# A two-row product with a long contraction, spread over four strips of output partitions

## The chip, the cores and the metric

The kernel runs on one core of one Trainium2 chip. The metric is device time in microseconds (us). Of each version several executions are timed, and one execution is profiled.

## The reference

Two transformer blocks are computed one after the other on 256 tokens of width 1024, all in float32. The first has three mixers (latent attention "MLA", gated linear attention "GLA", attention over a memory) and a feed-forward part; the second is modulated by a conditioning vector. The change touches only the modulation of the second block:

```python
mod = jax.nn.silu(c) @ w_mod[l] + b_mod[l]
shift1, scale1, gate1, shift2, scale2, gate2 = jnp.split(mod[:, None, :], N_MOD, axis=-1)
n_mod_c = 2 if last else N_MOD
mod_c = jax.nn.silu(c_ctx) @ w_mod[l, :, :n_mod_c * D_MODEL] + b_mod[l, :n_mod_c * D_MODEL]
mods_c = jnp.split(mod_c, n_mod_c)
h_c = ctx * (1.0 + mods_c[1]) + mods_c[0]
...
h = x * (1.0 + scale1) + shift1
```

`w_mod` is 1024 x 6144. Its first 2048 columns are wanted for two vectors (`c` and `c_ctx`), the other 4096 for one.

## The kernel before

Every engine has its own program, and semaphores tie them together. The order of the work on each engine is written out by hand.

**Weight panels.** A panel is 512 columns of a weight matrix. It goes through in units of two blocks of 128 rows: SP loads a unit into `raw` (a ring of four), ACT rounds it to `whi` (line 1228), DVE takes the rest as `wlo` (line 1645), and PE (line 703) multiplies both with the split activations into one of two `acc` banks. One unit is 12 matmuls with 512 columns each. ACT and DVE run three units ahead of PE.

**Modulation panels.** The 6144 columns of `w_mod` are 12 panels. POOL loads each in four pieces into `wm` (line 599), one piece as soon as `mod_free` says that it was used; loads of the first five panels stand ahead of POOL's rotary work in its program. `sic` holds both conditioning vectors as columns (128 partitions, 8 blocks for each). The first four panels are done on PE by `mod_panel`: for each of the 8 blocks of the contraction, a matmul with the two columns of `sic` as its stationary side and 128 x 512 of `wm` as its moving side adds into partitions 0 and 1 of a PSUM bank (`turned`). DVE copies the two rows to `modrow` (`mod_row`, line 1732), PE turns them into columns (`mod_turn`, four transposes with 2 x 128 as the stationary side, line 788), and DVE adds the bias (`mod_out`, lines 1766 and 1767). The other eight panels are summed on DVE (`mod_sum_tile`) and PE turns their sums by matmuls with 128 x 128 as the stationary side and a column of ones, `one_col`, as the moving side (`mod_columns`, line 1030).

**Where the first four panels stand.** They lie in the loop of the GLA stage, over nine steps s = 0 to 8. On PE a step is: wait until `gla_in` is s; eight score matmuls of 128 columns each (line 897, step 1 line 889); two units of the panels Q1, Q2, G20, G21 (not in step 8); then `mod_panel(s // 2)` in the odd steps and `mod_turn(s // 2 - 1)` in the even ones from 2 on. On DVE a step s is: a split (line 1645), `decayed(s)` (lines 2025 and 2027, it needs the scores of step s - 1 and ACT's exponential for s, and signals `gla_in`), `weights(s - 1)` (line 2043, two masked copies), `exponents(s + 1)` (lines 2009 and 2010), a split, the gates G20 and G21 in steps 6 to 8 (`gate_in_psum` line 1974, `gate_on` line 1983), then `mod_row` in even and `mod_out` in odd steps. ACT's step is a cast, the exponential (line 1390), a cast, an evacuation or a sigmoid (lines 1246 and 1373), and from step 5 on eight sums of squares (line 1411). After the loop come `mod_out(3)` and `weights(8)` on DVE, the products with the GLA values on PE (lines 916 and 917), ACT's root of the query norms (line 1260), the panels UKV0 to UKV3 and the MLA stage.

Of the kernel before, what the change touches and what calls it, by code (L numbers as in the profile page):

```python
# [25 lines left out]
ALU = mybir.AluOpType  # L26
ACT = mybir.ActivationFunctionType
AX = mybir.AxisListType

P = 128  # L30
# [3 lines left out]
KT = D // P  # L34
# [24 lines left out]
COLS = 512  # L59
# [3 lines left out]
class Order:  # L63
# [5 lines left out]
    def done(self, ins):  # L69

        self.n += 1
        ins.then_inc(self.sem, 1)
        self.eng.wait_ge(self.sem, self.n if self.i is None else self.n + self.per * self.i)
# [59 lines left out]
AB_KEYS, AB_QUERIES, AB_OUT = 12, 13, 18  # L133
AB_GATE = 2
MOD_CTX = 4
MOD_LOOP = 3
MOD_UNIT = 3
MOD_DOWN = (2, 8, 17, 21, 26)
# [23 lines left out]
def t_names():  # L162
# [8 lines left out]
    out += g("y", 4) + g("hc", 4) + g("h2", 4)  # L171
    out += [f"WU{c}.{i}" for c in range(8) for i in range(2)] + g("mod", 12)[MOD_CTX:]
    out += g("x2", 4) + g("kA", 2) + g("qA", 2)
# [26 lines left out]
def hybrid_kernel(nc, a, out):  # L200

    ctx = ExitStack()
    with ctx:
        def sem(name):
            return ctx.enter_context(nc.semaphore(name))

        def sb(name, shape, dt=F32, scope=ctx):
            return scope.enter_context(nc.sbuf_tensor(name, shape, dt))
# [3 lines left out]
        tb = [ctx.enter_context(nc.psum_tensor(f"turned{i}", [P, COLS], F32)) for i in range(2)]  # L212
# [8 lines left out]
        ident = sb("ident", [P, P])  # L221
# [5 lines left out]
        modx = sb("modx", [P, 16])  # L227
        ln1c = sb("ln1c", [P, 16])
        x3c = sb("x3c", [P, 16])
        one_col = sb("one_col", [P, 1])  # L230
        sic = sb("sic", [P, 16])
        rot = sb("rot", [P, 2, T, 64])
        bias = sb("bias", [P, 2, COLS])
        wm = sb("wm", [P, KT // UNIT, UNIT, COLS])
        modrow = sb("modrow", [2, COLS])
        turn = sb("turn", [P, 2, COLS])
        prob = sb("prob", [P, 2, COLS])
        probT = sb("probT", [P, 2, COLS])
# [106 lines left out]
        t_free = [sem(f"turned_free{i}") for i in range(2)]  # L345
# [16 lines left out]
        def ev(name):  # L362

            if name not in once:
                once[name] = sem(name)
            return once[name]
# [319 lines left out]
        def _(pe):  # L686
# [28 lines left out]
            def t_begin(name):  # L715
                b, k = T_USE[name]
                pe.wait_ge(t_free[b], k + 1)
                return tb[b], t_full[b]
# [49 lines left out]
            def mod_panel(c):  # L768

                bank, full = t_begin(f"mod.{c}")  # L770
                if c == 0:
                    pe.wait_ge(ev("sic_ready"), 1)
                pe.wait_ge(mod_free, 4 * c + 4)
                for k in range(KT // UNIT):
                    pe.wait_ge(mod_landed[k], 16 * (c + 1))
                    for kk in range(UNIT):
                        kt = UNIT * k + kk
                        ins = pe.matmul(bank[0:2, :], sic[:, kt:kt + KT + 1:KT], wm[:, k, kk],  # L778
                                        start=(kt == 0), stop=(kt == KT - 1))
                    ins.then_inc(mod_free if kt < KT - 1 else full, 1)  # L780

            def mod_turn(c):

                b, k = T_USE[f"mod.{c}"]
                pe.wait_ge(t_free[b], k + 2)
                bank, full = t_begin(f"modt.{c}")
                for j in range(4):
                    ins = pe.transpose(bank[:, 2 * j:2 * j + 2], modrow[:, P * j:P * j + P], ident[0:2, 0:2])
                ins.then_inc(full, 1)

            def lt_wait(name, g=3):
# [31 lines left out]
            s, k = PLAN.bank("AQ")  # L823
            pe.wait_ge(panel_out[s], k + 2)
            bank, full = t_begin("aT")
            for t in range(T):
                ins = pe.transpose(bank[:, P * t:P * t + P], aq[:, t, 0:P], ident[:])
            ins.then_inc(full, 1)
            panel("GQ", lta)
            b, k = T_USE["aT"]  # L830
            pe.wait_ge(t_free[b], k + 2)
            pe.wait_ge(ev("wg_landed"), 16)
            for g in range(2):
                bank, full = t_begin(f"z.{g}")
                for j in range(2):
                    h = 2 * g + j
                    ins = pe.matmul(bank[:, 256 * j:256 * j + 256], wg[0:GATE_RANK, P * h:P * h + P],
                                    aT[0:GATE_RANK, :], start=True, stop=True)
# [10 lines left out]
            for name in ("mqT", "mkT"):  # L849
                b, k = T_USE[name]  # L850
# [27 lines left out]
            for g in ("gqT.0", "gqT.1", "gkT.0", "gkT.1"):  # L878
                b, k = T_USE[g]
                pe.wait_ge(t_free[b], k + 2)  # L880
            qg = ["Q1", "Q2", "G20", "G21"]
            for s in range(9):
# [3 lines left out]
                if s == 1:  # L886
                    bank, full = s_begin("gla.off")
                    for h in range(H_GLA):
                        ins = pe.matmul(bank[:, P * h:P * h + P], lhs[:, h, 0:P], rhs[:, h, P:2 * P],
                                        start=True, stop=True)  # L890
                    ins.then_inc(full, 1)
                else:
                    for t in range(T):
                        bank, full = s_begin(f"gla.{max(s - 1, 0)}.{t}")
                        for h in range(H_GLA):
                            tok = slice(P * t, P * t + P)
                            ins = pe.matmul(bank[:, P * h:P * h + P], lhs[:, h, tok], rhs[:, h, tok],  # L897
                                            start=True, stop=True)
# [7 lines left out]
            for name in ("gla.off", "gla.7.0", "gla.7.1"):  # L906
                b, k = S_USE[name]
                pe.wait_ge(s_free[b], k + 2)
            for t in range(T):
                for g in range(2):  # L910
                    bank, full = t_begin(f"go.{2 * t + g}")
                    for j in range(2):
                        h = 2 * g + j
                        o = bank[:, 256 * j:256 * j + 256]
                        if t == 1:
                            pe.matmul(o, attn[:, 2, h, :], gv[:, 0, 256 * h:256 * h + 256], start=True, stop=False)
                        ins = pe.matmul(o, attn[:, t, h, :], gv[:, t, 256 * h:256 * h + 256],
                                        start=(t == 0), stop=True)
# [8 lines left out]
            for g in range(4):  # L927
                bank, full = t_begin(f"qn.{g}")
                for j in range(2):
                    for t in range(T):  # L930
                        c = 192 * (2 * g + j)
                        ins = pe.transpose(bank[:, 256 * j + P * t:256 * j + P * t + P], q[:, t, c:c + P], ident[:])
# [3 lines left out]
            for g in range(2):  # L936
                bank, full = t_begin(f"qr.{g}")
                for j in range(2):
                    for t in range(T):
                        ins = pe.transpose(bank[:, 256 * j + P * t:256 * j + P * t + P],  # L940
                                           work[:, t, 0:512][:, P * (2 * g + j):P * (2 * g + j) + P], ident[:])
                ins.then_inc(full, 1)
            bank, full = t_begin("kp")
            for t in range(T):
                ins = pe.transpose(bank[:, P * t:P * t + P], kpe[:, t, :], ident[:])
            ins.then_inc(full, 1)
            pe.wait_ge(ev("k_normed"), 1)
            for g in range(4):
                bank, full = t_begin(f"kn.{g}")
                for j in range(2):  # L950
                    for t in range(T):
                        c = 256 * (2 * g + j)
                        ins = pe.transpose(bank[:, 256 * j + P * t:256 * j + P * t + P], kv[:, t, c:c + P], ident[:])
                ins.then_inc(full, 1)
            for g in ("kn.2", "kn.3"):
                b, k = T_USE[g]
# [66 lines left out]
            def mod_columns(c):  # L1023

                bank, full = t_begin(f"mod.{c}")
                n = c - MOD_CTX
                pe.wait_ge(mod_sum, n + 1)
                src = msum[0][:, n] if n < MOD_LOOP else msum[1][:, n % 2]
                for j in range(4):
# [4 lines left out]
            for c in range(2):  # L1034
                for k in range(D_FF // P // UNIT):
                    if c == 0 and k == 2:
                        up_turn(7)
                    n = units_of("WD0") * c + k
                    if 0 <= n - MOD_UNIT < MOD_LOOP:
                        mod_columns(MOD_CTX + n - MOD_UNIT)  # L1040
                    if n == 2 * units_of("WD0") - 1:
# [4 lines left out]
                    if n in MOD_TURN:  # L1046
                        mod_columns(MOD_CTX + MOD_LOOP + MOD_TURN.index(n))
                    if c == 0 and k % 2 == 0:
                        for g in range(2):
                            b, n = T_USE[f"WU{k // 2}.{g}"]  # L1050
# [4 lines left out]
            for k in range(4):  # L1055
                if k == 1:
                    p, n = PLAN.bank("WD1")
# [573 lines left out]
        def _(dve):  # L1631
            order = Order(dve, dve_order)
            done = order.done
# [94 lines left out]
            def mod_row(c):  # L1728

                b, k = T_USE[f"mod.{c}"]  # L1730
                dve.wait_ge(t_full[b], k + 1)
                dve.tensor_copy(modrow[:], tb[b][0:2, :]).then_inc(t_free[b], 1)
                dve.sem_inc(mod_free, 1)

            def mod_sum_tile(total, kt, c):
# [13 lines left out]
            def mod_sums(c, pos):  # L1749

                n = c - MOD_CTX
                if n >= MOD_LOOP + 2:
                    b, k = T_USE[f"mod.{c - 2}"]
# [6 lines left out]
            def mod_out(c):  # L1760

                b, k = T_USE[f"mod.{c}" if c >= MOD_CTX else f"modt.{c}"]
                dve.wait_ge(t_full[b], k + 1)
# [66 lines left out]


            dve.wait_ge(ev("grid_ready"), 1)
            dve.wait_ge(ev("pos_landed"), 16)
            done(dve.tensor_copy(stat[:, 7, 6:8], stat[:, 7, 4:6].bitcast(I32)))
            done(dve.tensor_copy(stat[:, 7, 8:9], stat[:, 7, 2:3].bitcast(I32)))
# [41 lines left out]
            b, k = T_USE["h.3"]  # L1877
# [18 lines left out]
            for g in range(2):  # L1896
                b, k = T_USE[f"z.{g}"]
                dve.wait_ge(t_full[b], k + 1)
                for j in range(2):
                    ins = dve.tensor_scalar(zb[:, 2 * g + j, :], tb[b][:, 256 * j:256 * j + 256],  # L1900
                                            col("b_gla_gate", 2 * g + j), None, ALU.add)
# [24 lines left out]
            b, k = T_USE["ck"]  # L1926
            dve.wait_ge(t_full[b], k + 1)
            for kk in range(2):
                ins = dve.tensor_scalar(turn[:, 0, 256 * kk:256 * kk + 256], tb[b][:, 256 * kk:256 * kk + 256],
                                        col("g_ckv", kk), None, ALU.mult)  # L1930
# [118 lines left out]
            for g in ("gqT.0", "gqT.1", "gkT.0", "gkT.1"):  # L2049
                b, k = T_USE[g]  # L2050
# [47 lines left out]
            for t in range(T):  # L2098
                for h in range(H_GLA):
                    v = r_gla[:, t, DV_GLA * h:DV_GLA * h + DV_GLA]  # L2100
                    ins = dve.scalar_tensor_tensor(v, og[:, t, h], stat[:, 6, 4 * t + h:4 * t + h + 1], v, ALU.mult, ALU.mult)
# [39 lines left out]
            for c in range(2):  # L2141
                name, part = f"WO{c}", slice(COLS * c, COLS * c + COLS)
                p = panel_wait(name)
# [37 lines left out]
            assert cursor[0] == u0 + AHEAD  # L2181
            with dve.Fori(0, MOD_LOOP) as i:
                order.enter(i, KT)
                for c in (1, 2):
# [5 lines left out]
                    up_square(c, i)  # L2190
                order.leave(MOD_LOOP)
            cursor[0] += 24
# [6 lines left out]
            for c in range(2):  # L2199
# [14 lines left out]
                p = panel_wait(name)  # L2214
# [135 lines left out]
            for g in range(2):  # L2350
                b, k = T_USE[f"gate2.{g}"]
# [4 lines left out]
            for half in (slice(0, COLS), slice(COLS, D)):  # L2356
                for t in range(T):
                    ins = dve.tensor_scalar(x[:, t, half], x[:, t, half], stat[:, 1, 2 + t:3 + t], stat[:, 1, 4 + t:5 + t],
                                            ALU.add, ALU.mult)
# [83 lines left out]
```

## Time and profile before

| | |
|---|---|
| median of 3 executions | 1028.32 us (1028.26 to 1030.88) |
| profiled execution, span | 1025.4 us |
| its own time | not recorded apart; the median lies 2.9 us above the span |
| PE busy | 977.8 us (95%) |
| weight loads of PE | 765.0 us (75%) |
| DVE busy | 747.6 us (73%) |
| ACT busy | 551.8 us (54%) |
| POOL busy | 168.8 us (16%) |
| HBM read | 173.33 MB, 170 GB/s over the span |

The span is the time from the first to the last instruction of the profiled execution. PE is TensorE's matmuls, PEld its weight loads, which can overlap them. The chain of waits is followed back from the last instruction: at each step to what released it, or to the instruction before it on its engine. A group of matmuls in the profile counts instructions: a float32 product is two of them, each with a weight load of its own, a transpose is one. Ends of matmuls are modelled, so the time that a row of them takes is read from start to start.

### The profile page before, as it was taken

The page shows a single profiled execution, that of the slowest core. Times are in us where ns is not written, and L with a number is a line of the kernel's source. Part 1 is how long each engine was busy: PE and PEld are TensorE (multiplying, and loading weights), DVE is VectorE, ACT ScalarE, POOL GpSimd, SP SyncE. Part 2 cuts the span into 40 slices and gives each one's busy share as a digit, 9 for nine tenths or more (in the row PEclk, how much of TensorE's full clock was granted, in tenths as well). Part 3 has the DMA queues.
Part 4 walks back from the last instruction along what each step waited for, and adds up shares of the span by engine and source line. Part 5 has one row for each costly group of instructions (what it writes and reads, how often), then busy time and mean ns, then how long its engine had stood idle before and what let it go on. Part 6 is the DMA issues. An engine that isn't in the chain of part 4 may idle for free.

```text
span 1025.4 us, 13780 instructions
## 1 busy us (share of the span) xinstructions
PE 977.8 (95%) x4636; PEld 765.0 (75%) x4636; DVE 747.6 (73%) x1085; ACT 551.8 (54%) x816; POOL 168.8 (16%) x250
## 2 busy tenths in 40 slices
PE   6999999999999999999999999999999799999995
PEld 5787785665867787888888887776777578777784
DVE  5778456676667778887678787666567879999945
ACT  6557545264766445555333336756543467777532
POOL 7000000113600000110112002450000323333400
PEclk9999999999999999999999999999999899999998
DMA  8675454665543156887589555211125355556551
GB/s 257 212 242 164 123 165 155 217 201 156 158 156 108 63 175 211 266 264 242 200 306 339 180 179 191 73 62 62 62 76 183 91 158 169 166 171 218 181 189 41
DMA packets 99746, 175.11 MB, mean 171 GB/s; under 512 B 8252, under 2 KB 36444, under 8 KB 99692
## 3 DMA queue, kind: packets, MB, share of 16 engines
q1 hardware_dynamic: 92460, 148.87, 45.8%
q0 software_dynamic: 7184, 25.50, 7.7%
q8 instruction: 32, 0.52, 0.2%
q14 instruction: 22, 0.18, 0.1%
q10 hardware_dynamic: 48, 0.04, 0.0%
HBM read 173.33 MB, written 1.05 MB: 170 GB/s over the span
## 4 chain that ended last, share of the span: by engine, by line
PE 81%; DVE 10%; ACT 5%; issue 4%; DMA 1%; DVEq 0%; SPq 0%; ACTq 0%
PE acc L703 61%; PE scores L1103 3%; PE turned L778 3%; PE turned L1111 2%; DVE wlo L1645 2%; PE turned L755 2%; PE scores L897 2%; ACT whi L1228 1%; DVE ltb_lo L1685 1%; PE turned L729 1%; PE scores L964 1%; DVE conv L2379 1%; DVE turn L1700 1%; PE scores L963 1%; DVE turn L1703 1%
## 5 line engine op out<-in xcount | busy, mean ns | idle before, releaser
L1645 DVE TENSOR_TENSOR wlo<-raw,whi 128x1024 fp32r<-128x1024 f32 (+2 forms) x270 | 347.1, 1306 | 104.9 <-ACT whi L1228 96.1
L1228 ACT CAST whi<-raw 128x1024 fp32r<-128x1024 f32 (+2 forms) x270 | 273.5, 1030 | 206.6 <-PE acc L703 171.1
L703 PE MATMUL acc<-whi,lta_lo 128*128 128x512 f32 (+2 forms) x576 | 229.0, 398 | 4.5 <-DVE lta_lo L1685 3.6
L703 PE MATMUL acc<-wlo,lta_hi 128*128 128x512 f32 (+2 forms) x576 | 223.2, 387 | 0.0
L703 PE MATMUL acc<-whi,lta_hi 128*128 128x512 f32 (+2 forms) x576 | 223.1, 387 | 0.0
L703 PEld LDWEIGHTS acc<-whi,lta_lo 128*128 128x128 f32 x576 | 108.9, 189 | 39.3 <-issue 13.5
L703 PEld LDWEIGHTS acc<-wlo,lta_hi 128*128 128x128 f32 x576 | 109.0, 189 | 22.4
L703 PEld LDWEIGHTS acc<-whi,lta_hi 128*128 128x128 f32 x576 | 109.0, 189 | 19.9
L703 PE MATMUL acc<-whi,ltb_lo 128*128 128x512 f32 (+1 forms) x272 | 109.7, 403 | 6.8 <-DVE ltb_lo L1685 3.5
L599 POOL DMA_DIRECT2D wm<-in_w_mod x48 | 34.5, 719 | 478.6 <-DVEq L1745 264.8
L703 PE MATMUL acc<-whi,ltb_hi 128*128 128x512 f32 (+1 forms) x272 | 106.7, 392 | 0.0
L703 PE MATMUL acc<-wlo,ltb_hi 128*128 128x512 f32 (+1 forms) x272 | 106.3, 391 | 0.0
L703 PEld LDWEIGHTS acc<-whi,ltb_lo 128*128 128x128 f32 x272 | 52.0, 191 | 23.2 <-DVE ltb_lo L1685 4.9
L1266 ACT ACTIVATE probT<-turned 128x512 f32<-128x512 f32 (+1 forms) x44 | 25.3, 576 | 66.9 <-PE turned L755 66.7
L703 PEld LDWEIGHTS acc<-wlo,ltb_hi 128*128 128x128 f32 x272 | 52.0, 191 | 11.8
L703 PEld LDWEIGHTS acc<-whi,ltb_hi 128*128 128x128 f32 x272 | 52.1, 192 | 10.2
L703 PE MATMUL acc<-whi,ff_lo 128*128 128x512 f32 x128 | 51.3, 401 | 0.0
L703 PE MATMUL acc<-whi,ff_hi 128*128 128x512 f32 x128 | 50.5, 395 | 0.0
L703 PE MATMUL acc<-wlo,ff_hi 128*128 128x512 f32 x128 | 50.5, 395 | 0.0
L703 PE MATMUL acc<-whi,act_lo 128*128 128x512 f32 x88 | 34.9, 397 | 0.1
L703 PE MATMUL acc<-whi,act_hi 128*128 128x512 f32 x88 | 34.8, 395 | 0.0
L703 PE MATMUL acc<-wlo,act_hi 128*128 128x512 f32 x88 | 34.7, 395 | 0.0
(340 smaller groups left out, 1429.5 us busy)
## 6 DMA issues: line engine op xcount, KB each, us to landing
raw<-in_w_in SPq DMA_DIRECT2D x88, 512.0 KB, 4.2
wm<-in_w_mod POOLq DMA_DIRECT2D x48, 512.0 KB, 5.2
raw<-in_w_up SPq DMA_DIRECT2D x88, 256.0 KB, 3.2
raw<-in_w_up SPq DMA_DIRECT2D x32, 512.0 KB, 4.7
raw<-in_w_down SPq DMA_DIRECT2D x32, 512.0 KB, 5.0
raw<-in_w_down SPq DMA_DIRECT2D x44, 256.0 KB, 3.0
raw<-in_w_mem_kv SPq DMA_DIRECT2D x8, 512.0 KB, 6.2
raw<-in_w_o SPq DMA_DIRECT2D x8, 512.0 KB, 3.6
```

Of the source, the lines that this page charges most:

```text
L599: pool.dma_start(wm[:, k], rows(a["w_mod_2"], k)[:, :, bass.ds(COLS * c, COLS)])\
L703: ins = pe.matmul(acc[s][:, t, 0:n], lhs[part][:, kt0 + kk, tok], w[:, u % RING, kk, 0:n], start=(k == 0 and kk == 0 and j == 0), stop=(la ...
L729: ins = pe.transpose(bank[:, 256 * kk + P * t:256 * kk + P * t + P], src[:, t, c:c + P], ident[:])
L755: ins = pe.transpose(bank[:, P * j:P * j + P], prob[:, (STEPS[name][0] + i) % 2, P * j:P * j + P], ident[:])
L778: ins = pe.matmul(bank[0:2, :], sic[:, kt:kt + KT + 1:KT], wm[:, k, kk], start=(kt == 0), stop=(kt == KT - 1))
L897: ins = pe.matmul(bank[:, P * h:P * h + P], lhs[:, h, tok], rhs[:, h, tok], start=True, stop=True)
L963: pe.matmul(o, qnT[:, h, P * t:P * t + P], knT[:, h, 0:P * (t + 1)], start=True, stop=False)
L1103: return pe.matmul(bank[:, :], qT[br][lane, h // 2, P * t:P * t + P], kT[br][lane, h // GROUP, :], start=True, stop=True)
L1111: ins = pe.matmul(bank[:, 0:HD], pT[:, P * kt:P * kt + P], v[:, HD * (h // GROUP):][:, 0:HD], start=(kt == 0), stop=(kt == 3))
L1228: act.copy(whi[:, s, :, 0:n], raw[:, s, :, 0:n]).then_inc(hi_ready, 1)
L1266: act.activation(dst, tb[b][0:(parts or P), 0:n], ACT.Copy, scale=scale).then_inc(t_free[b], 1)
L1645: dve.tensor_tensor(wlo[:, s, :, 0:n], raw[:, s, :, 0:n], whi[:, s, :, 0:n].bitcast(F32), ALU.subtract)\
```

## The change

The matmuls of block kt of a modulation panel write to partitions 32 * (kt mod 4) and the one after it instead of always to partitions 0 and 1. The blocks 0 to 3 start the four sums and the blocks 4 to 7 end them. So a panel ends as four partial sums of two rows each, in partitions 0, 1, 32, 33, 64, 65, 96 and 97. `modrow` is 98 partitions high and `mod_row` copies all 98 rows (of the rows between, whatever the bank holds). `mod_turn` is four float32 matmuls instead of four transposes: the stationary side is 98 x 128 of `modrow`, the moving side is `strips`, 98 x 2 zeros and ones that add the four partial sums. `strips` is built once from the identity by a DVE reduction near the start, and shares a small tile with `one_col`.

```diff
+STRIPS = 4
+STRIP_ROWS = 32 * (STRIPS - 1) + 2
...
-        one_col = sb("one_col", [P, 1])
+        strip_cols = sb("strip_cols", [P, 3])
+        one_col, strips = strip_cols[:, 0:1], strip_cols[:, 1:3]
...
-        modrow = sb("modrow", [2, COLS])
+        modrow = sb("modrow", [STRIP_ROWS, COLS])
...
                         kt = UNIT * k + kk
-                        ins = pe.matmul(bank[0:2, :], sic[:, kt:kt + KT + 1:KT], wm[:, k, kk],
-                                        start=(kt == 0), stop=(kt == KT - 1))
+                        row = 32 * (kt % STRIPS)
+                        ins = pe.matmul(bank[row:row + 2, :], sic[:, kt:kt + KT + 1:KT], wm[:, k, kk],
+                                        start=(kt < STRIPS), stop=(kt >= KT - STRIPS))
...
                 for j in range(4):
-                    ins = pe.transpose(bank[:, 2 * j:2 * j + 2], modrow[:, P * j:P * j + P], ident[0:2, 0:2])
+                    ins = pe.matmul(bank[:, 2 * j:2 * j + 2], modrow[:, P * j:P * j + P], strips[0:STRIP_ROWS, :],
+                                    start=True, stop=True)
...
-                dve.tensor_copy(modrow[:], tb[b][0:2, :]).then_inc(t_free[b], 1)
+                dve.tensor_copy(modrow[:], tb[b][0:STRIP_ROWS, :]).then_inc(t_free[b], 1)
...
             dve.wait_ge(ev("grid_ready"), 1)
+            done(dve.tensor_reduce(strips[:], ident[:].rearrange("p (g c) -> p c g", g=STRIPS)[:, 0:2, :], AX.X, ALU.add))
             dve.wait_ge(ev("pos_landed"), 16)
```

## Rows read from the trace of the kernel before

**Rows 1.** The page: the span, and the chain that ended last, by engine and line.

```profile
span 1025.4 us, 13780 instructions
...
PE 81%; DVE 10%; ACT 5%; issue 4%; DMA 1%; DVEq 0%; SPq 0%; ACTq 0%
PE acc L703 61%; PE scores L1103 3%; PE turned L778 3%; PE turned L1111 2%; DVE wlo L1645 2%; PE turned L755 2%; PE scores L897 2%; ACT whi L1228 1%; DVE ltb_lo L1685 1%; PE turned L729 1%; PE scores L964 1%; DVE conv L2379 1%; DVE turn L1700 1%; PE scores L963 1%; DVE turn L1703 1%
```

**Rows 2.** Chain of waits in the GLA loop and behind it: start us, us, what.

```profile
172.94 6.96 PE turned L778 x16
179.90 1.98 PE scores L897 x16
181.88 5.46 PE acc L703 x24
187.34 0.34 PE turned L788 x4
...
239.59 6.96 PE turned L778 x16
...
251.03 1.96 PE turned L917 x8
```

**Rows 3.** Line 778: durations (least, median, most), first and last start, forms.

```profile
L778 PEld LDWEIGHTS turned<-wm,sic x64: 82/85/86, 172.9 to 245.5; 128*2 128x2 f32 x64
L778 PE MATMUL turned<-wm,sic x64: 592/592/593, 172.9 to 246.0; 128*2 128x512 f32 x64
```

**Rows 4.** Timeline of PE's weight loads inside the first modulation panel.

```profile
172.87 0.09 PEld L778 LDWEIGHTS turned<-wm,sic 128*2 128x2 f32 x2 [0.35 <-issue]
173.30 0.09 PEld L778 LDWEIGHTS turned<-wm,sic 128*2 128x2 f32 x1 [0.34 <-issue]
```

**Rows 5.** Chain of waits around `mod_columns`, and line 1030's weight loads on the timeline.

```profile
492.48 0.79 PE turned L1030 x8
...
495.78 1.09 PEld L1030 LDWEIGHTS turned<-one_col,work 128*128 128x128 f32 x8
```

**Rows 6.** Chain of waits: products of one tile shape (917, 916), and of alternating shapes (963, 964).

```profile
254.38 0.43 PE turned L917 x2
...
299.27 0.63 PE scores L964 x2
```

**Rows 7.** Timeline of DVE, GLA steps 4 to 8.

```profile
202.13 0.68 DVE L1732 COPY modrow<-turned 2x512 f32<-2x512 f32 x1 [6.88 <-PE turned L778]
...
226.34 0.69 DVE L2025 TENSOR_TENSOR arena<-arena 128x512 f32<-128x512 f32 x1 [0.17 <-PE scores L897]
...
234.59 0.69 DVE L2025 TENSOR_TENSOR arena<-arena 128x512 f32<-128x512 f32 x1
...
236.03 1.51 DVE L2043 COPY_PREDICATED arena<-gmask,scores 128x512 f32<-128x512 int8 x2
```

**Rows 8.** Timeline of ACT: the exponential of step 7.

```profile
224.84 1.06 ACT L1390 ACTIVATE arena<-arena 128x1024 f32<-128x1024 f32 x1
```

**Rows 9.** Stages of two loop steps: PE, PEld, DVE, ACT, POOL busy, PEclk, DMA share, GB/s.

```profile
179.90:187.70 7.80, 7.80 (x46) 6.56 (x45) 7.19 (x9) 1.32 (x2) 0.72 (x1) 1.00 0.73 258
187.70:195.10 7.40, 7.40 (x41) 6.16 (x42) 6.67 (x10) 2.79 (x3) 0.00 (x0) 1.00 0.46 142
195.10:202.10 7.00, 7.00 (x18) 1.32 (x17) 0.16 (x1) 2.91 (x3) 2.12 (x3) 1.00 0.72 200
```

**Rows 10.** A DMA issue group of the GLA stage (KB each, us to landing), and one issue on POOL's timeline.

```profile
wm<-in_w_mod POOLq DMA_DIRECT2D x16, 512.0 KB, 5.1
...
199.31 0.72 POOL L599 DMA_DIRECT2D wm<-in_w_mod  x1 [1.00 <-PE turned L778]
```

**Rows 11.** Near the start: a small DVE reduction, DVE's rotary work, ACT's sine.

```profile
L1719 DVE TENSOR_REDUCE stat<-work x8: 220/420/421, 54.1 to 64.1; 128x4 f32<-128x256 f32 x4, 128x1 f32<-128x256 f32 x2, 128x1 f32<-128x64 f32 x2
...
33.67 0.23 DVE L1855 TENSOR_SCALAR rot<-arena 128x128 f32<-128x128 f32 x1
...
37.33 1.28 ACT L1318 ACT_TABLE_LOAD   x1
```

## The prediction

> **What bounds the kernel now.** I first read the page. The chain that ended last is PE for 81% of a span of 1025.4 us, and line 778, the matmuls of the modulation panels, holds 3% of it [rows 1]. So these matmuls are on the path, not beside it. Then I read the chain of waits through the GLA loop [rows 2]. It never leaves PE: scores, two units, panel, scores, two units, turn, and so on, each piece starting where the last one ended. The panel at 172.94 holds the path for 6.96 us and so does the one at 239.59, the last of four of them: 27.8 us. A turn (line 788) holds it for 0.34 us. Behind the loop the chain goes through DVE's last work to the products of line 917 at 251.03. The table by stages says why nothing else shows: in a pair of steps (stages from 179.9 to 202.1) PE has no gap, DVE is nearly full in the steps without a panel (7.19 of 7.80 us) and idle under the panel (0.16 of 7.00) [rows 9]. Whatever shortens the panel is gained at once, until DVE or ACT are late.
>
> **What one panel consists of.** Line 778 is 64 instructions for 32 products [rows 3]: each float32 product is two instructions, each with its weight load. The weight loads come 0.43 us apart [rows 4], and 6.96 / 16 = 0.435 us is what one instruction takes from start to start (its own 592 ns is a modelled end). A weight load takes 85 ns and lies under the running matmul. All 16 use partitions 0 and 1 as output and can only follow each other.
>
> **The panel with four strips.** The number of instructions, their columns and their kind stay; only the output partitions turn. No pair of matmuls in this trace has different output strips, so whether they run side by side isn't shown. Bounds: if they run side by side without limit, four strips share 16 instructions, 4 x 0.435 = 1.74 us; if not at all, 6.96 us; if each change of strip has to empty the array as a change of tile shape does, more. The price of such a change can be read: two instructions with 256 columns take 0.43 us where shapes stay the same (lines 917, 916) and 0.63 us where 128-row and 64-row tiles alternate (lines 963, 964) [rows 6], so 0.20 us; eight changes make 1.60 us and the panel 8.56 us.
> I take a value between these. The two instructions of one product stand next to each other and go to the same strip, so the second has to wait for the first. If matmuls start in the order of the program, the next strip's first instruction starts beside the second instruction of the strip before, and no earlier. Each product then costs one slot of 0.435 us instead of two, with one slot more at the end: 9 x 0.435 = 3.92 us. If the weight loads of 85 ns can't be hidden any more when two are wanted in a slot, the slot is 0.52 us and the panel 8 x 0.52 + 0.435 = 4.60 us. So 3.92 us saves 3.04 us a panel, 12.2 us for four; 4.60 us would save 9.4 us.
> The order of starts is only argued here. The Trainium skill (TensorE: Matmul & The Clock Gate, Part 3: Packing small matmuls) says that matmuls are in program order in start and end, and gives 2.38 times for three column strips; its table has no word on float32 products of two instructions. By that rate alone a panel would be 6.96 / 2.38 = 2.92 us and the time about 1014 us, an estimate between my value and full overlap. No run here shows it.
>
> **The turn.** Before: four transposes, one instruction each, 0.34 us on the path [rows 2]. After: four float32 products with a stationary side of 98 x 128, so eight instructions and eight weight loads of 128 columns. `mod_columns` is the same form (128 x 128 stationary, one column moving, eight instructions) and holds the path for 0.79 us [rows 5]. The turn costs 0.79 - 0.34 = 0.45 us more, four times on the path: +1.8 us. Bounds: 0 more, and 0.75 more if all of the 1.09 us of its eight weight loads showed [rows 5]. I take the row of the same form.
>
> **Parts that I cost at nothing.** `mod_row` copies 98 partitions instead of two; the 512 elements of a partition are the same and it takes 0.68 us before [rows 7]. It lies under PE's scores and units; without that cover it would be 0.68 us a panel, as before. The build of `strips` is one DVE reduction of 128 x 8 elements; the nearest are 0.22 to 0.42 us [rows 11]. It pushes back DVE's rotary work, which ends at 33.9 us, while ACT comes to the sine at 37.33 [rows 11]: 3.4 us of cover, and 0.4 us at most if that were gone. POOL's loads keep their order and bytes. Each now waits for a pair of blocks that is done in about half the time; an issue takes 0.72 us and POOL idles 1.00 us before it [rows 10], so the four still go out one by one, and POOL's rotary work behind the fifth panel starts earlier with them. A load lands after 5.1 us [rows 10], the next panel comes some 19 us later. The pair of steps moves 201 GB/s on average ((7.8 x 258 + 7.4 x 142 + 7.0 x 200) / 22.2); in 22.2 - 2.6 = 19.6 us it would be 228 GB/s, under the 258 that the first of these stages already reaches [rows 9].
>
> **Does DVE or ACT become late?** DVE stands idle for 6.88 us before `mod_row`, until the panel ends [rows 7], so with a panel of 3.92 us its earlier work is still done in time; and `decayed` then starts 0.17 us after its scores, so `mod_row` and a split fit under the scores as they do now. One place needs care: ACT's exponential of step 7 runs from 224.84 to 225.90 [rows 8] behind a sigmoid, eight sums of squares and a table load, none of which waits for the panel. With 3.04 us less the scores of step 6 end at 223.3 and `decayed` of step 7 starts at about 226.0 instead of 226.34; two multiplies later, at 227.4, `gla_in` is 7, and PE, after two units (5.46) and a turn (0.79), asks for it at 221.3 + 1.98 + 5.46 + 0.79 = 229.5. That leaves 2.1 us. The next, `decayed(8)`, starts at 234.3 instead of 234.59 [rows 7] and is wanted after panel 3, near 240.5. DVE's gate addition in step 8 waits for the two units before panel 3 and ends under that panel. So 4 x (3.04 - 0.45) = 10.4 us go through. After the loop all is tied by semaphores alone, and moves up as a block.
>
> **The sum.** Span 1025.4 - 12.2 + 1.8 = 1015.0 us; the median of the executions lies 2.9 us above the span, so 1017.9, rounded to 1018 us.
>
> **Rivals.**
> *Full overlap.* If the two instructions of a product don't hold back the next strips, a panel is 1.74 us and saves 4.77 us net. The first two give 9.5 us. In the second pair ACT's exponential and then DVE's row of decayed(8), weights, split, gate addition, `mod_row`, turn, `mod_out`, weights(8) set the end: from 234.3 on that is 1.45 + 1.5 + 1.2 + 1.25 + 0.7 + 0.8 + 0.4 + 1.5 = 8.8 (two multiplies of 0.69, masked copies of 1.51 [rows 7], the rest estimates of the same sizes), so line 917 starts near 243.3 instead of 251.03, 7.7 us. Together 17.2 us: 1011 us. For it: the strips are independent. Against: it needs matmuls that overtake one that waits.
> *No overlap.* The array takes one moving stream at a time; panels stay at 6.96 us, turns cost 1.8 us: 1030.1 us, within 0.3%. For it: nothing in the trace shows two matmuls side by side; even the 64-row tiles of line 964 don't share time with line 963 (they couldn't, as line 963 uses all rows).
> *Each strip change empties the array.* 4 x (1.60 + 0.45) = 8.2 us more: 1036.5 us. It decides for slower from 0.04 us a change on (3.1 / 4 = 0.78, less 0.45, by 8). For it: the 0.20 us of alternating shapes [rows 6]. Against: the shape of the tile stays the same from strip to strip.
> Beside it: the Trainium skill (TensorEngine Tiling (Array Packing), Key Properties) says that a change of the mode empties the array and a change of the tile alone does not; the 0.20 us agree with its first half, no row shows the second.
> *Overlap is there, but the loads or DVE take half of it*: 1023 us.
>
> **How the numbers follow.** Half overlap 0.42, full 0.18, none 0.25, emptying 0.08, half of it lost elsewhere 0.07. The likeliest gives 1018 us; its own range is 1014 (the turn free, panel 3.9) to 1022 (slot of 0.52 us and a turn at 1.09). The range of 8 in 10 holds both signs: 1010, the full overlap, to 1031, no overlap with the turns dear; it leaves out the emptying. What a measurement of this kernel can tell from no change is about 0.3%, 3.1 us. Faster: 0.42 + 0.18 + 0.06 = 0.66; the same: 0.26; slower: 0.08.
>
> **What the profile after would show.** Line 778: still 64 matmuls, but pieces of 3.9 us in the chain of waits (1.7, 7.0 or 8.6 by the rivals), with the first instruction of one strip starting together with the second of the strip before. Line 788: 32 instructions, 0.79 us a piece. Line 2025 of step 7 waiting for ACT, the others for PE. Scores of steps 5 and 7 still start without a wait on PE. The start of line 917 near 240.6. The prediction is wrong if matmuls of different strips start one after the other, or all together.

## The result, and the profile after

| | before | after |
|---|---|---|
| median, same chip | 1029.60 us (4 executions, 1028.26 to 1033.32) | 1013.12 us (4 executions, 1010.30 to 1014.43) |
| ratio | | 0.9831, interval 0.9803 to 0.9858 |
| profiled execution, span | 1025.4 us | 1011.1 us |
| the profiled execution's own time | not recorded apart | 1012.67 us |

The kernel is 1.7% faster: the medians differ by 16.5 us, the profiled spans by 14.3. I had forecast 1018 us for the likeliest case and 1011 us for full overlap. 1013.12 lies inside the range, and much nearer to the second.

The page of the kernel after, the chain that ended last. Line 778 is now 782, 703 is 706, 788 is 792, 917 is 922:

```profile
span 1011.1 us, 13813 instructions
...
PE 75%; DVE 13%; ACT 6%; issue 5%; DMA 2%; DVEq 0%; SPq 0%; ACTq 0%
```

PE's share of the chain fell from 81% [rows 1] to 75%, and DVE's rose to 13%. The modulation panels are gone from its first places. The chain of waits in the GLA loop (start us, us, what) answers to [rows 2]:

```profile
174.10 1.83 PE turned L782 x16
175.93 1.98 PE scores L902 x16
177.91 5.46 PE acc L706 x24
183.37 0.79 PE turned L792 x8
...
195.32 2.77 PE acc L706 x12
...
216.08 1.07 ACT arena L1395
...
217.25 0.70 DVE arena L2031
...
231.01 0.70 DVE modrow L1737
...
231.75 1.07 PE turned L792 x8
...
233.24 0.74 DVE arena L2049
234.00 0.74 DVE arena L2049
234.74 0.25 issue
234.98 3.75 PE turned L922 x8
```

A panel holds the path for 1.83 us instead of 6.96, and a turn for 0.79 instead of 0.34. Behind the first unit of step 4 (195.32 and 2.77 us) the chain leaves PE for ACT and DVE and comes back to it at 231.75. PE itself first stands idle before the scores of step 7:

```profile
219.58 2.02 PE L902 MATMUL scores<-arena 128*128 128x128 f32 x16 [0.56 <-DVE arena L2049]
```

The eight matmuls of line 922 take 3.75 us, which took 1.96 us before [rows 2]. Line 782 asked for alone, in two stretches inside the first panel (durations in ns, first and last start):

```profile
L782 PEld LDWEIGHTS turned<-wm,sic x8: 82/84/86, 174.0 to 174.1; 128*2 128x2 f32 x8
L782 PE MATMUL turned<-wm,sic x4: 592/592/593, 174.0 to 174.0; 128*2 128x512 f32 x4
...
L782 PE MATMUL turned<-wm,sic x8: 592/592/593, 174.0 to 174.5; 128*2 128x512 f32 x8
```

Four matmuls start together at 174.0, the next four start together 0.43 us later. Two of the first four instructions in the program belong to each of strips 0 and 1, so the four that start together can't be the first four of the program: the first halves of products 2 and 3 started beside product 0's, past waiting second halves of the products before them. (Instructions of one strip start 0.43 us apart, never together [rows 4].) The Trainium skill (TensorE: Matmul & The Clock Gate, Part 3: Packing small matmuls) has matmuls in program order in start and end; this row differs from it for the start, and the measurement decides.

ACT and DVE around step 7, on their timelines:

```profile
210.47 1.01 ACT L1378 ACTIVATE acc<-acc 128x1024 f32<-128x1024 f32 x1 [1.81 <-DVE acc L1980]
211.39 0.30 ACT L1416 ACTIVATE prob<-arena 128x128 f32<-128x128 f32 x1
...
214.78 1.28 ACT L1395 ACT_TABLE_LOAD   x1
216.08 1.06 ACT L1395 ACTIVATE arena<-arena 128x1024 f32<-128x1024 f32 x1
```

```profile
210.86 0.69 DVE L1737 COPY modrow<-turned 98x512 f32<-98x512 f32 x1 [0.42 <-PE turned L782]
217.25 0.69 DVE L2031 TENSOR_TENSOR arena<-arena 128x512 f32<-128x512 f32 x1 [1.22 <-ACT arena L1395]
```

The copy of 98 rows takes 0.69 us, the copy of two took 0.68 [rows 7]. Line 2031 (2025 before) now waits for ACT's exponential, where it waited for PE before [rows 7, 8].

The span splits where PE's programs are the same on both sides. Stretch A runs from the first matmul of the first modulation panel to the first of line 917 or 922; stretch B from there to the first MLA score:

| kernel | A | B | A + B |
|---|---|---|---|
| before | 78.2 | 46.7 | 124.9 |
| after | 61.0 | 49.2 | 110.2 |

A lost 17.2 us, B gained 2.5. Ahead of A the kernel after was 1.2 us later, behind the start of the MLA scores 0.8 us shorter, both of which also differ between executions of one kernel. -17.2 + 2.5 + 1.2 - 0.8 = -14.3 us, the difference of the spans. Why B grew shows in the table by stages of the kernel after (us, then PE, PEld, DVE, ACT, POOL busy, granted clock, DMA share, GB/s):

```profile
231.00:235.00 4.00, 1.07 (x9) 1.02 (x9) 2.68 (x7) 3.98 (x18) 2.82 (x8) 0.78 1.01 381
235.00:239.00 4.00, 4.00 (x10) 3.19 (x11) 3.75 (x6) 1.17 (x4) 3.15 (x6) 0.50 0.85 304
239.00:243.00 4.00, 4.00 (x18) 3.44 (x17) 2.26 (x1) 1.00 (x3) 3.92 (x2) 0.86 0.01 4
```

PE stood idle for most of 231 to 235, and the granted clock, on average 0.78 there, is 0.50, the level of 1.2 GHz, for 235 to 239.

### The profile page after: what moved, and what is told of

Its sections match the earlier page's. It is cut to its first block, busy times and chain, and to the rows that moved or that the text cites. A ratio compares the mean times of both kernels' runs of the same rounds, so it can differ in the third digit from the quotient of the medians.

```text
span 1011.1 us, 13813 instructions
## 1 busy us (share of the span) xinstructions
PE 961.3 (95%) x4652; PEld 766.0 (76%) x4652; DVE 747.0 (74%) x1086; ACT 551.7 (55%) x816; POOL 168.2 (17%) x250
## 4 chain that ended last, share of the span: by engine, by line
PE 75%; DVE 13%; ACT 6%; issue 5%; DMA 2%; DVEq 0%; SPq 0%; ACTq 0%
PE acc L706 58%; DVE wlo L1650 3%; PE scores L1108 3%; PE turned L1116 3%; PE turned L758 2%; ACT whi L1233 2%; DVE ltb_lo L1690 1%; DMA raw<-in_w_mem_kv 1%; PE turned L732 1%; DVE turn L1705 1%; PE scores L969 1%; PE scores L902 1%; DVE conv L2385 1%; PE scores L968 1%; DVE turn L1708 1%
## 5 line engine op out<-in xcount | busy, mean ns | idle before, releaser
L1233 ACT CAST whi<-raw 128x1024 fp32r<-128x1024 f32 (+2 forms) x270 | 273.5, 1030 | 193.0 <-PE acc L706 148.7
```

The lines of the kernel that those rows point to most:

```text
L1233: act.copy(whi[:, s, :, 0:n], raw[:, s, :, 0:n]).then_inc(hi_ready, 1)
```

## The experiments

The theories were **A**, strips run beside each other and an instruction can start past others that wait for their own strip, and **B**, matmuls start in program order (my prediction). A second question was what limits the last two panels, and a third what the clock costs. In this section "ratio" is to the kernel before on the same chip, with its interval.

**The changed kernel once more.**

> The changed kernel once more, on the chip of the next three, so that they can be compared with it. Both theories: a panel of 1.83 us in the chain of waits, about 16 us less than before (ratio near 0.983).

1012.19 us, ratio 0.9835 (0.9802 to 0.9868), A 61.0, B 49.5. The stretches repeat to 0.3 us, the medians to 1 us. So I read the small terms from the stretches.

**One strip, new copy and new turn.**

```diff
-                        row = 32 * (kt % STRIPS)
+                        row = 0
...
-                                        start=(kt < STRIPS), stop=(kt >= KT - STRIPS))
+                                        start=(kt == 0), stop=(kt == KT - 1))
...
-                    ins = pe.matmul(bank[:, 2 * j:2 * j + 2], modrow[:, P * j:P * j + P], strips[0:STRIP_ROWS, :],
+                    ins = pe.matmul(bank[:, 2 * j:2 * j + 2], modrow[:, P * j:P * j + P], ident[0:STRIP_ROWS, 0:2],
```

> One strip as before, but the copy of 98 rows and the turn by matmuls. Theory A (strips run beside each other, and even a strip whose turn has not come in program order is started) and theory B (matmuls start in program order, so that the second instruction of a product holds back the next strip) say the same here: panels of 6.96 us, turns of 0.79 us instead of 0.34, 1.8 us more than before (ratio 1.0018). If the new turn cost more than its own 0.45 us, for one by a change of tile shape, it would be 3 us or more.

1032.15 us, ratio 1.0020 (1.0003 to 1.0038). Its chain of waits:

```profile
174.27 6.96 PE turned L782 x16
...
188.68 0.79 PE turned L792 x8
...
253.85 2.44 PE turned L922 x8
```

A is 79.7, 1.5 us over before (I had 1.8). The whole gain is the strips' and the turn costs what line 1030 cost. B is 48.3, 1.6 us more than before, because the clock fell behind the loop here too (2.44 us for eight matmuls); I had not expected that.

**Two blocks in a row on each strip.**

```diff
-                        row = 32 * (kt % STRIPS)
+                        row = 32 * (kt // 2)
...
-                                        start=(kt < STRIPS), stop=(kt >= KT - STRIPS))
+                                        start=(kt % 2 == 0), stop=(kt % 2 == 1))
```

> Four strips, but two consecutive blocks go to the same strip (0 0 1 1 2 2 3 3), so that four instructions in a row share a strip. Theory A, with a look-ahead over the whole panel: 4 slots of 0.435 us, a panel of 1.8 us, the time of the changed kernel (16 us less than before). Theory B, starts in program order: only the last instruction of a strip overlaps the first of the next, 13 slots, 5.65 us a panel, 4 x (6.96 - 5.65 - 0.45) = 3.4 us less than before. In between: a look-ahead that is shorter than the panel, 2 to 5 us a panel.

1013.66 us, ratio 0.9835 (0.9802 to 0.9868), A 61.0.

```profile
174.91 1.85 PE turned L782 x16
```

```profile
174.84 0.13 PEld L782 LDWEIGHTS turned<-wm,sic 128*2 128x2 f32 x8 [0.35 <-issue]
175.27 0.12 PEld L782 LDWEIGHTS turned<-wm,sic 128*2 128x2 f32 x4 [0.30 <-issue]
175.70 0.12 PEld L782 LDWEIGHTS turned<-wm,sic 128*2 128x2 f32 x4 [0.30 <-issue]
```

The first row is the chain's, the others PE's weight loads on the timeline. The panel takes 1.85 us where theory B asks for 5.65. Here the thirteenth instruction is the first of strip 3. Eight weight loads go at once, where one strip alone has two at once [rows 4], so all four strips are at work from the start. Theory B is refuted.

**Two strips in turn.**

```diff
-                        row = 32 * (kt % STRIPS)
+                        row = 64 * (kt % 2)
...
-                                        start=(kt < STRIPS), stop=(kt >= KT - STRIPS))
+                                        start=(kt < 2), stop=(kt >= KT - 2))
...
-            done(dve.tensor_reduce(strips[:], ident[:].rearrange("p (g c) -> p c g", g=STRIPS)[:, 0:2, :], AX.X, ALU.add))
+            done(dve.tensor_reduce(strips[:], ident[:].rearrange("p (g c) -> p c g", g=2)[:, 0:2, :], AX.X, ALU.add))
```

> Two strips in turn (partitions 0 and 64). Theory A: 16 instructions over 2 strips, 8 slots, 3.5 to 3.6 us a panel, 4 x (6.96 - 3.57 - 0.45) = 11.8 us less than before. Theory B: 9 slots, 3.92 us, 10.4 us less. If the array were one stream of data that only happens to be short here, the panel would stay near 6.96.

1017.82 us, ratio 0.9876 (0.9842 to 0.9909), A 65.9, B 46.8.

```profile
173.06 3.53 PE turned L782 x16
```

3.53 us is 8 slots of 0.435 and 0.05: theory A to 0.05 us. A is 12.2 us below before, 11.8 expected. All of it arrives, so with 3.53 us a panel neither ACT nor DVE is late, as the prediction had it for 3.92.

**Halves: blocks 0 to 3 on one strip, 4 to 7 on the other.**

```diff
-                        row = 32 * (kt % STRIPS)
+                        row = 64 * (kt // 4)
...
-                                        start=(kt < STRIPS), stop=(kt >= KT - STRIPS))
+                                        start=(kt % 4 == 0), stop=(kt % 4 == 3))
...
-            done(dve.tensor_reduce(strips[:], ident[:].rearrange("p (g c) -> p c g", g=STRIPS)[:, 0:2, :], AX.X, ALU.add))
+            done(dve.tensor_reduce(strips[:], ident[:].rearrange("p (g c) -> p c g", g=2)[:, 0:2, :], AX.X, ALU.add))
```

> Two strips, the first four blocks on one and the last four on the other, so eight instructions in a row share a strip. If the second strip's first instruction can start although seven before it still wait (look-ahead of eight instructions or more), the panel is 3.5 us as with two strips in turn. If the look-ahead is four instructions, which the four strips in pairs would allow only in part, it is 4.4 to 5.3 us; starts in program order would give 15 slots, 6.5 us.

One execution: 1024.05 us, A 72.8, B 48.3.

```profile
174.53 5.25 PE turned L782 x16
```

```profile
174.46 0.09 PEld L782 LDWEIGHTS turned<-wm,sic 128*2 128x2 f32 x2 [0.35 <-issue]
...
175.75 0.09 PEld L782 LDWEIGHTS turned<-wm,sic 128*2 128x2 f32 x1 [0.34 <-issue]
176.18 0.09 PEld L782 LDWEIGHTS turned<-wm,sic 128*2 128x2 f32 x3 [0.34 <-issue]
176.61 0.09 PEld L782 LDWEIGHTS turned<-wm,sic 128*2 128x2 f32 x2 [0.34 <-issue]
```

5.25 us is 12 slots of 0.435: for four slots strip 0 works alone, and after its first two weight loads one follows in each slot (174.90, 175.32, 175.75); then three loads come at once at 176.18 and both strips run. So the second strip's first instruction, the ninth, started beside the fifth, past three that waited. In the run with pairs the thirteenth started beside the first, past nine that waited, but never more than three for the same strip. Both fit a queue of four for each strip (one running, three waiting) and an order that is kept only within a strip. That form is inferred from these two runs and not tested further; that there is a limit, and that it isn't a plain count of instructions, is shown.

**Strips in the first two panels only, and in the last two only.** The other panels and turns are those of before; both copy 98 rows in all four panels.

```diff
-                        row = 32 * (kt % STRIPS)
+                        n = STRIPS if c < 2 else 1
+                        row = 32 * (kt % n)
...
-                                        start=(kt < STRIPS), stop=(kt >= KT - STRIPS))
+                                        start=(kt < n), stop=(kt >= KT - n))
...
```

> Four strips and the new turn in the first two panels only (steps 1 and 3), the last two as before. In the first two panels nothing but PE sets the path, so 2 x (6.96 - 1.83 - 0.45) = 9.4 us less than before, and no fall of the granted clock behind the loop (line 922's first eight matmuls in 1.96 us). If DVE or ACT were late there too, it would be under 8 us.

> Four strips and the new turn in the last two panels only (steps 5 and 7). Theory: ACT's exponential of step 7 and then DVE's row of work set the end of the loop, which takes 1.5 us of the 9.4, and the idle PE behind the loop lets the clock fall to 0.50, which costs 2.4 us: about 5.3 us less than before, with line 922's first eight matmuls in 3.75 us. Rival: the clock fell for the sum of all four panels (less PE work over a longer time); then the eight take 1.96 us here and the kernel is 7.8 us faster than before.

First two: 1020.22 us, ratio 0.9911 (0.9881 to 0.9941), A 68.5, 9.6 us less than before (9.4 expected); B 48.4, since the clock fell here as well, against my expectation. So A + B is 7.9 us less than before, of the 9.4 expected. Last two (`c >= 2` in the diff): 1022.42 us, ratio 0.9922 (0.9893 to 0.9951), A 70.9, 7.3 us less than before (7.9 expected); B 49.6, and A + B 4.4 us less (5.3 expected). 9.6 + 7.3 = 16.9, the changed kernel has 17.2: the two halves add up, and the last two panels give 2.3 us less than the first two. The chains' rows of the eight matmuls behind the loop, first two and last two:

```profile
242.33 3.09 PE turned L926 x8
```

```profile
244.21 3.75 PE turned L926 x8
```

The rival in the second expectation, that the clock falls only with all four panels, is out: these eight matmuls (line 922, here 926) took 3.75 us with the last two alone.

**The squares of a step behind the next exponential.** Only ACT's order changes.

```diff
+            def query_squares(s):
                 if s >= 5:
...
                 act.activation(e, e, ACT.Exp).then_inc(ev("gla_expd"), 1)
+                query_squares(s - 1)
...
+            query_squares(8)
```

> The changed kernel with ACT's eight sums of squares of a GLA step moved behind the exponential of the next step. If these squares (2.3 us) are what makes the exponential of step 7 late, it starts about 2 us earlier and the stretch from the first panel to line 921 falls from 61.0 us by 1 to 2.3 us. If DVE's own row of work sets the end of the loop, it stays at 61.0.

1010.58 us, ratio 0.9816 (0.9778 to 0.9854). The chain of waits from step 6 to the panel of step 7, and the products behind the loop:

```profile
212.39 1.98 PE scores L902 x16
214.37 5.48 PE acc L706 x24
219.86 0.79 PE turned L792 x8
220.64 1.89 PE scores L902 x16
222.54 5.45 PE acc L706 x24
227.99 1.83 PE turned L782 x16
...
234.76 2.94 PE turned L922 x8
```

The chain is back on PE throughout the loop, and A falls from 61.0 to 59.1, by 1.9 us. The eight sums of squares ahead of the exponential were what held the last two panels back. DVE's own row of work did not. Behind the loop the clock fell here too: 2.94 us for the eight matmuls, B 48.3.

**Ten products of the identity in the wait before line 921.** They are extra work with an unused result.

```diff
+            s, cnt = PLAN.bank("UKV0")
+            pe.wait_ge(panel_out[s], cnt + 1)
+            for j in range(10):
+                pe.matmul(acc[s][:, 0, 0:P], ident[:], ident[:], start=True, stop=True)
             for name in ("gla.off", "gla.7.0", "gla.7.1"):
```

> The changed kernel with ten 128 x 128 products of the identity (2.1 us on PE, result unused) in the wait before line 921. If the fall of the clock is due to that wait of 2.18 us, after 0.89 us more shortly before, it stays at 1.00, line 922's first eight take 1.96 us again and the whole is about 2.4 us faster than the changed kernel (18 to 19 us less than before). If the clock falls for another reason, the time is that of the changed kernel.

1011.47 us, ratio 0.9825 (0.9779 to 0.9871): beside 1013.12 and 1012.19 the medians alone settle nothing. The timeline does (line 922 is 926 here):

```profile
231.65 2.48 PE L914 MATMUL acc<-ident 128*128 128x128 f32 x20
233.99 1.96 PE L926 MATMUL turned<-arena 128*128 128x256 f32 x8
```

With PE kept at work the eight matmuls take 1.96 us again, A stays at 61.0 and B is 46.8, where the kernel before has 46.7. So the clock accounts for 2.4 of the 2.5 us of stretch B.

**Real work in the same place.**

```diff
+            pe.wait_ge(ev("ckT_ready"), 1)
+            unit("UKV0", 0, ckT)
             for name in ("gla.off", "gla.7.0", "gla.7.1"):
...
-            for c in range(4):
+            for c in range(1, 4):
                 unit(f"UKV{c}", 0, ckT)
```

> The changed kernel with the unit of panel UKV0 (twelve matmuls, 2.8 us of real work) moved into the wait before line 921. It takes 2.8 us out of the chain after it, delays line 922 by some 0.4 us and keeps the clock at 1.00 (2.4 us): 4 to 5 us faster than the changed kernel, near 1008 us. If the clock still falls, 2.4 us faster; if what follows waits for DVE or POOL and not for PE, nothing of the moved work is gained and only the clock's 2.4 us, or less, is.

1008.53 us, ratio 0.9799 (0.9749 to 0.9849). A 61.5, B 44.5: A + B is 106.0, 4.2 us less than after, of the 4 to 5 expected.

**All together.** The squares moved, UKV0's unit before the last `mod_turn`, and on DVE `weights(8)` before `mod_out(3)`:

```diff
                 elif s >= 2:
+                    if s == 8:
+                        pe.wait_ge(ev("ckT_ready"), 1)
+                        unit("UKV0", 0, ckT)
                     mod_turn(s // 2 - 1)
...
-            mod_out(3)
             weights(8)
+            mod_out(3)
```

> The squares moved as in the run beside it, UKV0's unit put before the last turn, and DVE's masked copies for step 8 before its last mod_out. UKV0 takes 2.8 us out of the chain and keeps the clock up, the order on DVE 1 us, the squares 1 to 2: 6 to 8 us less than the changed kernel, 22 to 24 less than before (ratio 0.977). If the squares give nothing, 21 less.

1007.20 us (1004.92 to 1009.49), ratio 0.9779 (0.9737 to 0.9820), A 59.6, B 44.2.

```profile
228.35 1.98 PE scores L902 x16
230.34 2.79 PE acc L706 x12
233.12 0.79 PE turned L792 x8
233.91 1.83 PE turned L925 x8
```

PE goes from the scores through UKV0 and the turn into the products (line 925 here) without a gap. A + B is 103.8, 6.4 us less than after (6 to 8 expected); against before the medians say 21.1 us, a little less than the 22 to 24 expected. It has the lowest median of the study, though its interval overlaps that of the run with UKV0 early alone. The profiled spans differ by less, 1007.9 against 1011.1: behind the start of the MLA scores this execution takes 729.9 us against 726.9, and the clock, which stayed up behind the loop, is low farther on, in a stage where the kernel after has 1.00:

```profile
281.00:287.00 6.00, 6.00 (x14) 3.81 (x13) 3.85 (x8) 1.85 (x5) 0.00 (x0) 0.50 0.31 92
```

So not all of what the stretches gain arrives in every execution.

**The kernel before, once more.**

> The kernel before, profiled once more, for the clock alone. If a given idle time of PE (2.18 us before line 916) always leads to the same clock, the eight matmuls of line 917 take 1.96 us and the clock stays at 1.00 there, as in its first profile. If it depends on where the idle time falls, as the one-strip kernel with the new turn suggests (2.44 us with the same idle time), they may take longer here, and the comparison of single executions carries an uncertainty of 2 to 3 us.

One execution: 1032.60 us, span 1031.0, A 78.2, B 46.8: the clock stayed at 1.00 at line 917 here too. Farther on it was low in another place. The stage from 302 to 308 of this execution, and the same of the first profile of before:

```profile
302.00:308.00 6.00, 6.00 (x13) 3.92 (x14) 4.15 (x8) 1.84 (x5) 0.00 (x0) 0.50 0.28 87
```

```profile
302.00:308.00 6.00, 6.00 (x27) 4.42 (x28) 4.33 (x9) 3.91 (x10) 0.00 (x0) 1.00 0.26 83
```

## Why the prediction was half right

**The time.** 1013.12 us lies inside the range of 1010 to 1031 because that range was drawn around every case but the emptying; the likeliest case, 1018, rested on an order of starts that the kernel doesn't have. Its own range began at 1014 for a free turn and a panel of 3.9 us, but that sum is 1025.4 - 12.2 + 2.9 = 1016.1.

**The path.** Right. The panels were on it, the strips shortened it at once, and nothing downstream gave the time back except through the clock.

**The panel.** Here the prediction failed, at the step "If matmuls start in the order of the program, the next strip's first instruction starts beside the second instruction of the strip before, and no earlier". I took 9 slots, 3.92 us; it is 4 slots and 0.09, 1.83 us. With pairs it is still 1.85 us where the order of starts would give 5.65, so the order isn't kept between strips; on one strip the instructions still follow each other, one slot apart. The prediction named "all together" as a sign of being wrong, and four matmuls do start together; it had given full overlap a chance of 0.18. The factor for four strips is 6.96 / 1.83 = 3.8, above the 2.38 that the Trainium skill (TensorE: Matmul & The Clock Gate, Part 3: Packing small matmuls) gives for three. The slot of 0.435 us held: 3.53 us is 8 slots for two strips in turn, 5.25 us is 12 for the halves.

**No drain.** The rival that each strip change empties the array (0.20 us each) is refuted: 4 x 0.435 = 1.74 leaves 0.09 us for the whole panel. The Trainium skill's rule (TensorEngine Tiling (Array Packing), Key Properties) that changing the tile alone doesn't drain agrees with these 0.09 us.

**The turn.** Right in form: 0.79 us in the chain for steps 2 to 6, as read from line 1030. Four of them cost 1.5 us in stretch A against 1.8.

**DVE and ACT.** The forecast that they stay in time was made for 3.92 us, and two strips at 3.53 us bear it out. For 1.83 us the rival "full overlap" had worked out 9.5 us for the first two panels and 7.7 for the last two: 17.2 in the loop. Measured: 9.6 and 7.3 apart, 17.2 together. The place was right (ACT's exponential of step 7); I had put part of the blame on DVE's row, and moving ACT's squares alone gave back 1.9 us and put PE on the path again. The forecast that the scores of steps 5 and 7 start without a wait failed for step 7, by 0.56 us.

**What no case held.** The clock. The full-overlap rival said 1011 us from a span of 1025.4 - 17.2, and 2.4 us of clock behind the loop make 1013.6; measured 1013.12. That this comes so near is in part luck, since the profiled spans differ by 14.3 us and the medians by 16.5. The prediction's likeliest case took 10.4 us off where the loop gave 17.2 and stretch B took 2.5 back.

**The parts at nothing.** The copy took 0.69 us and stayed under PE's scores except in step 8, where line 792 waited 0.89 us for it: DVE's gate addition ahead of it ended at 230.87, not under the panel as forecast. `strips`, POOL's loads and the transfers cost nothing that shows: the busiest stage reached 381 GB/s, and no row of line 706 in the loop waits for a transfer.

## What to carry to other kernels

A product with few output rows (two here) leaves room for others beside it: send the blocks of its contraction to different output strips, add the strips up in the product that turns them anyway, and the panel shrinks almost by the number of strips. Lay out the order so that no strip is given more than a few instructions in a row: four in a row cost nothing here, eight did. In every layout run here the last instruction of the panel, which alone signals its end, lay on a strip that finished last; no run shows whether one signal is enough where another strip would finish later. When a piece of the path gets short, look for the engine that was hidden behind it (here ACT's squares before an exponential that DVE waits for), and put real work of PE into the wait that opens up, since the granted clock may fall there and slow what follows.

## What the runs showed of the hardware that I had not expected

Matmuls of different output strips pass each other: the thirteenth instruction of a panel started beside the first (weight loads eight at once at 174.84), but the ninth only beside the fifth when the eight before it shared one strip (5.25 us a panel).

The clock's fall behind the loop does not follow from the idle time of that place alone. With 2.2 us of idle PE before lines 917 and 922 the clock stayed at 1.00 in both profiles of the kernel before and with two strips in turn, but fell in the one-strip kernel with the new turn (2.44 us for eight matmuls), with the halves (2.55), with the squares moved (2.94) and with strips in the first two panels (3.09); with 0.9 us more of idle time just ahead of it, it fell in all four profiles that have both (after, its repetition, the pairs, the last two panels; 3.75 us each). Nor does a clock that stays up there stay up for good: it was 0.50 from 281 to 287 us in the run with all together and from 289 to 295 with two strips in turn, where the part behind the start of the MLA scores took 729.9 and 730.1 us against 726.9 after. With the ten products of the identity (726.9) and with UKV0 early alone (725.8) no such cost followed. The kernel before met a low clock near 302 us in one execution and not in the other; their spans are 1031.0 and 1025.4, with A + B at 124.9 in both. What decides stays open. Single executions of this kernel differ by several us, which is why the small terms above are taken from stretches of the trace, not from medians.
